# A hybrid transformer block and a PEER block on one core: five weight subtractions moved from VectorE to GpSimd, norms moved later, and fifteen unread float32 products added on TensorE

## The reference, cut to what matters

```python
def reference(x, ...):
    x = first_block(x, ...)
    return second_block(x, ...)

# first_block: rmsnorm, u @ w_in; a gated delta rule with 4 heads in chunks
#   (a triangular solve in each) beside causal attention with 8 heads and a
#   forget gate; @ w_out; a swiglu with d_ff 2816; a last rmsnorm
# second_block:
h = modulate(rmsnorm_2(x, norm1_g), shift1, scale1)
proj = h @ w_in                       # q, k, v, and three inputs of a short convolution
attn = sliding_window_attention(rope(norm(q)), rope(norm(k)), v, sinks)
conv = cb * short_conv(cc * cu, conv_w)
x = x + gate1 * (concat(rmsnorm_2(attn), rmsnorm_2(conv)) @ w_out)
h2 = modulate(rmsnorm_2(x, norm2_g), shift2, scale2)
x = x + gate2 * peer(h2, ...)         # 8 heads, each picks 16 of 16384 experts per token
```

## Time and profile before

| | |
|---|---|
| median of 3 runs | 2389.42 us (2389.01 to 2391.6) |
| profiled execution | 2392.0 us, of which the span from first to last instruction is 2390.2 us |
| busy: PE, DVE, ACT, POOL | 2342.3, 1482.9, 909.6, 1100.0 us |

### The profile page before, as it was taken

One profiled execution on the slowest core, in us unless ns is written; L12 is line 12 of the kernel. 1 busy time (PEld: TensorE's weight loads), 2 busy tenths in 40 slices (PEclk: granted clock), 3 DMA queues, 4 the chain that ended last, 5 costly groups with the idle time before them and its releaser, 6 DMA issues.

```text
span 2390.2 us, 33961 instructions
## 1 busy us (share of the span) xinstructions
PE 2342.3 (98%) x11547; PEld 1490.9 (62%) x11547; DVE 1482.9 (62%) x2863; ACT 909.6 (38%) x1430; POOL 1100.0 (46%) x752
## 2 busy tenths in 40 slices
PE   8999899999999998998999999999999999999999
PEld 6888567668888876645864444444444566666665
DVE  4512367356968557645889885222222499899898
ACT  3222134232232352324345555454545433333332
POOL 0001121010000030002888888888888588886566
PEclk9999899999999999999999999999999999999999
DMA  7240454165656312212446666666667899999997
GB/s 210 71 73 1 155 199 144 70 189 167 210 160 194 88 53 71 71 37 87 89 98 147 157 147 157 146 157 146 157 146 157 276 409 363 373 369 379 369 360 285
DMA packets 437893, 426.51 MB, mean 178 GB/s; under 512 B 105000, under 2 KB 360104, under 8 KB 437680
## 3 DMA queue, kind: packets, MB, share of 16 engines
q1 hardware_dynamic: 353648, 332.85, 43.6%
q0 software_dynamic: 84160, 92.58, 15.5%
HBM read 364.28 MB, written 61.05 MB: 178 GB/s over the span
## 4 chain that ended last, share of the span: by engine, by line
PE 51%; POOL 26%; issue 5%; DVE 4%; ACT 1%; DMA 1%; SPq 0%; DVEq 0%; POOLq 0%; ACTq 0%
POOL dense_gates L868 26%; PE psum L1594 7%; PE psum L1596 7%; PE psum L1595 7%; PE psum L1288 5%; PE psum L1289 5%; PE psum L1290 5%; PE psum L1331 2%; PE psum L1051 1%; PE psum L1175 1%; PE psum L1277 1%; PE psum L1071 1%; PE psum L1131 1%; PE psum L1144 1%; PE psum L1344 1%
## 5 line engine op out<-in xcount | busy, mean ns | idle before, releaser
L868 POOL DMA_INDIRECT dense_gates<-arena x384 | 613.7, 1598 | 122.3 <-issue 116.7
L1571 PE MATMUL psum<-arena 128*128 128x512 bf16 x1024 | 389.8, 381 | 0.0
L1573 PE MATMUL psum<-arena 128*128 128x512 bf16 x1024 | 387.6, 379 | 0.0
L1572 PE MATMUL psum<-arena 128*128 128x512 bf16 x1024 | 387.0, 378 | 0.0
L2722 DVE TENSOR_TENSOR arena<-arena,psum 128x1024 bf16<-128x1024 f32 x124 | 151.5, 1222 | 335.5 <-ACT psum L2003 335.0
L1594 PE MATMUL psum<-arena,low 128*128 128x384 bf16 x1024 | 334.4, 327 | 0.9 <-DVE arena L2756 0.9
L1596 PE MATMUL psum<-arena,low 128*128 128x384 bf16 x1024 | 334.4, 327 | 0.0
L1595 PE MATMUL psum<-arena,low 128*128 128x384 bf16 x1024 | 334.4, 327 | 0.0
L2019 ACT ACTIVATE low<-low 128x1024 bf16<-128x1024 f32 x128 | 135.3, 1057 | 296.4 <-PE psum L1596 281.6
L888 POOL DMA_INDIRECT arena<-in_v,arena x128 | 182.8, 1428 | 75.9 <-DVE arena L2773 43.8
L896 POOL DMA_INDIRECT arena<-gelu_spill,arena x128 | 189.4, 1480 | 59.0 <-issue 36.6
(11 more groups left out here) (409 smaller groups left out, 4104.9 us busy)
## 6 DMA issues: line engine op xcount, KB each, us to landing
arena<-in_uT SPq DMA_DIRECT2D x128, 512.0 KB
low<-in_v SPq DMA_DIRECT2D x128, 512.0 KB, 5.5
gelu_spill<-cst SPq DMA_DIRECT2D x128, 256.0 KB, 3.2
dense_gates<-cst SPq DMA_DIRECT2D x16, 1536.0 KB, 10.3
arena<-in_ada_w POOLq DMA_DIRECT2D x12, 2048.0 KB, 9.0
arena<-gelu_spill SPq DMA_DIRECT2D x128, 192.0 KB, 5.8
arena<-dense_gates SPq DMA_DIRECT2D x128, 192.0 KB, 6.9
low<-in_w_in SPq DMA_DIRECT2D x20, 1024.0 KB, 7.3
```

The costliest lines, as they stand in the source:

```text
L868: pool.indirect_dma_start(gate_cells, bass.IndirectOffsetOnAxis(ap=cell_of[:, n:n + 1], axis=0), gate_of[:, n:n + 1], None, compute_op=ALU ...
L1571: mm(psum[:, bank, :], hi[:, c, :], h2hi[:, c, :], start=c == 0, stop=False)
L1572: mm(psum[:, bank, :], hi[:, c, :], h2lo[:, c, :], start=False, stop=False)
L1573: last = mm(psum[:, bank, :], lo[:, c, :], h2hi[:, c, :], start=False, stop=c == DC - 1)
```

## The change

Two things are changed.

First, `second_low(n)` for n = 0 to 4 goes from DVE to POOL: two ahead of POOL's operand lows and three behind them. PE waits for these on the semaphore g_rhs instead of x_nrm, whose count for n from 5 on is smaller by 5. On DVE the reciprocal of the last norm goes into step 1 of the window loop, and the eight `last_norm` calls go, two by two, into steps 2 to 5, each behind the step's last softmax instruction and ahead of its `second_low` calls.

Second, `keep_busy(bank, count, src)` issues `count` float32 products of 128x128 by 512 columns on constants (or on a tile of zeros at the first place) into a bank that is free there. Nobody reads them. There are six places: 3 behind the first `mean_square`; 1 ahead of item 4 and 2 ahead of item 5; 3 ahead of `first_pair`; 2 ahead of `half_mix`; 4 ahead of the PEER queries.

```diff
-            return S[name], {"x_exp": STEPS, "x_nrm": STEPS, "l2_sq": 2 * GH, ...
+            return S[name], {"x_exp": STEPS, "x_nrm": STEPS - 5, "g_rhs": 3 * NT, "l2_sq": 2 * GH, ...
...
@@ gpsimd
+            def second_low(n):
+                pool.wait_ge(*second_part("x_exp", n + 1))
+                pool.tensor_tensor(second_cols(n, slot_halves), second_cols(n, slot), s_high[n % 4], ALU.subtract
+                                  ).then_inc(S["g_rhs"], 1)
+            for n in range(2):
+                second_low(n)
             for c in range(LOWS_POOL):
                 pool.wait_ge(*second_part("l2_sq", c + 1))
                 pool.tensor_tensor(s_operand_low[c], u2[:, c, :], s_operand_high[c], ALU.subtract).then_inc(S["g_nm"], 1)
+            for n in range(2, 5):
+                second_low(n)
...
@@ tensor
+            def keep_busy(bank, count, src=cst[:, 0:SEC]):
+                for _ in range(count):
+                    mm(psum[:, bank, :], src[:, 0:P], src, start=True, stop=True)
...
             mean_square(0, HALF, [psum[:, 6, 0:HALF], psum[:, 7, 0:HALF]])
+            keep_busy(4, 3, gates[:, 0:SEC])
...
                 if what == "level" and a < len(ITEMS):
+                    if a in (4, 5):
+                        keep_busy(7, a - 3)
                     merge_p(a)
...
             mean_last(0, sq1, "sq1_ready", 0)
+            keep_busy(7, 3)
...
-                pe.wait_ge(*second_part("x_nrm", n + 1))
+                pe.wait_ge(*second_part("x_nrm" if n >= 5 else "g_rhs", n + 1))
...
             pe.wait_ge(*fill_done(F_OUT2))
+            keep_busy(2, 2)
...
             mean_last(3, u2)
+            keep_busy(7, 4)
...
@@ vector
             modulated(0, col_n1, DC)
-            for n in range(2):
-                second_low(n)
...
-            dve.wait_ge(S["std_ready"], 5)
-            settle(dve.reciprocal(r2[:, 1, :], r2[:, 1, :]))
...
-                if j < 4:
-                    last_norm(2 * j)
-                    last_norm(2 * j + 1)
-                if j == 0:
-                    second_low(2)
-            second_low(3)
-            second_low(4)
             rotate(4)
             second_low(5)
...
+                if s == 1:
+                    dve.wait_ge(S["std_ready"], 5)
+                    settle(dve.reciprocal(r2[:, 1, :], r2[:, 1, :]))
+                elif 2 <= s <= 5:
+                    last_norm(2 * s - 4)
+                    last_norm(2 * s - 3)
```

More of the change, by code:

```diff
@@ L451, in second_part @@
         def second_part(name, n):
-            return S[name], {"x_exp": STEPS, "x_nrm": STEPS, "l2_sq": 2 * GH, "l2_done": 2 * GH, "g_nm": len(ITEMS)}[name] + n
+            return S[name], {"x_exp": STEPS, "x_nrm": STEPS - 5, "g_rhs": 3 * NT, "l2_sq": 2 * GH, "l2_done": 2 * GH, "g_nm": len(ITEMS)}[name] + n
         def second_done(n):
```

## The result

The changed kernel took 2372.97 us (median of 4 runs, 2370.54 to 2374.15) against 2389.22 us for the kernel before (4 runs): ratio 0.9926, 95% interval 0.9911 to 0.9942. A second measurement gave 2372.72 us, ratio 0.9932 (0.9917 to 0.9948), where the kernel before took 2388.13. So it is faster, by 15 to 16 us. The profiled execution took 2370.54 us, 21.5 us less than the profiled one of before (2392.0). Why one pair of profiles says 21.5 and the medians say 16.3 is the main question of what follows.

The account below looks back on a forecast made before the run. PE bounds the kernel through a few waits and the clock falls around them (57 us at the lower clock). Terms sum to -23.6 us: 2392.0 profiled gives 2368.4, less 2.6 for the median 2365.8 us; range 2361 to 2380.

Parts of the forecast that it names:

- From profile to median: Last step of the sum: the median of plain runs lies 2.6 us below the profiled execution, so 2368.4 becomes 2365.8.
- Inversion, -12.9: Attention steps around items 4 and 5: with gaps filled the clock no longer falls, saving 12.9 us.
- rival 1: Clock falls in the inversion all the same, behind the unfilled 2.7 us gap; time 2378.7 us; chance 0.15.
- Start, -0.3: Kernel start: filler keeps the clock up, but weights still loading decide; gain 0.3 us, bounds -1.8 and 0.
- Relief, -9.6 (5.7, 1.9, 0.8, 1.2): Second block: wait before product 3 (5.7), its clock fall (1.9), second (0.8) and first (1.2) waits at L1361 shrink.
- the term of -1.2: First wait at L1361, 2.3 us: middle taken between full gain and none if POOL's lows 0 and 1 stop DVE.
- Rival 2: The next wait takes up the relief; only some 3 of 9.6 us come; 2372.4 us; chance 0.13.
- Window loop, 0: Second block's window loop: added reciprocal and norms stand behind the instruction PE waits for; cost 0.
- L1480, -1.8: Half mixes' gap: filling it saves half of 3.6 us at the lower clock, 1.8 us.
- L1506, 0: PEER queries and behind: PE's gain is waited away, since POOL's indirect-write queue does not move with PE's clock; 0.
- The last phase, +1.0: L1594: a gap of some 3 us may let the clock fall; priced +1.0 us, between 0 and 1.9.
- the prediction's own signs: Right: full clock 260 to 440, no L1344 wait above 1 us, last phase 24 us earlier; wrong: stretched u2, POOL waits.

Follow-up runs that it names:

- the fillers alone: Kernel before with unread products added only ahead of items 4 and 5 of the inversion (1 and 2): 2384.15 us, ratio 0.9973.
- the kernel with two lows back: Changed kernel with low parts 0 and 1 of the second block back on VectorE, 2 to 4 staying on POOL: 2369.73 us, ratio 0.9920.
- the norms alone: Changed kernel with all five low parts back on VectorE; reciprocal and norms stay in the window loop, all fillers stay: 2375.16 us, ratio 0.9941.
- The third profile of before: Kernel before, unchanged, run a third time for one more profile: 2385.9 us at clock 0.993.
- the five low parts alone: Changed kernel with reciprocal and eight norms back in the query and key rounds; low parts stay on POOL, fillers stay: 2381.20 us, ratio 0.9965.
- the kernel with the relief only: Changed kernel without any unread products; only low parts, reciprocal and norms moved: 2378.93 us, ratio 0.9954.

## Why the prediction was right, and what it missed

Predicted 2365.8 us, range 2361 to 2380; measured 2373.0. The direction and range hold, and the forecast gains 7 us too much. Against the profiled execution the sum was nearly right: 2368.4 forecast, 2370.5 measured. That it comes within 2.1 us is partly luck: to the first attention scores and through the inversion 2.5 us less were gained than forecast, in the relief 1.4 and in the window loop 0.9 less, ahead of the first write 0.7 more and behind it 2.0 more.

- **From profile to median.** This is the largest miss, 5.0 of the 7.2 us. The prediction took 2.6 us off, as if the changed kernel's median lay under its profile as the old one's did. The profile of before (2392.0) had the longest stretch at half clock of the three, the very thing that the change removes; the changed kernel's profile was the fastest of its four. How long that stretch is in the typical execution is not on record. The medians say what its cure is worth: 6.5 us alone, and all fillers on top of the relief bring 6.0 (2378.93 to 2372.97). A gain that removes a varying loss must be sized on the typical execution.
- **Inversion, -12.9.** Measured -11.1 in the ten steps of the pair and -0.9 in item 5's first products just ahead of them, and 1.7 lost again at 265 behind the gap without a filler, which rival 1 had named; but there the clock was back before 270.6, where a score product takes 1.12 us as before, so rival 1's price was wrong. At the median the fillers alone brought 6.5.
- **Start, -0.3.** About -0.4: the merge at 256.59 before stands at 256.18 after, though the clock is 1.00 from 20 to 40. Right, and leaving it out costs nothing that could be measured.
- **Relief, -9.6 (5.7, 1.9, 0.8, 1.2).** Measured -8.2. The 5.7 us wait and its fall went. The collision was as feared: both low parts stopped u2 (6.70 against 3.26 us), the first turn waits 1.8 of its 2.3 us, and 1.1 us of idle PE is new in the first products, so the term of -1.2 measured +0.6. By the exclusion rule of the Trainium skill (SBUF - State Buffer, "Who interferes with whom") the term was 0 instead of -1.2; the trace and the kernel with two lows back agree with it. Rival 2, that the next wait eats most of it, did not come.
- **How the relief is split.** The prediction gave the low parts 7.6 of the 9.6 us, as if by themselves. Alone they bring nothing (66.6 against 65.3), while the norms alone, priced at the other 2.0, bring 4.3.
- **Window loop, 0.** It is 109.1 against 108.2, and 108.2 to 108.3 in every profile with the norms outside the loop. The reciprocal and norms there cost PE 0.9 us, not 0. Its waits for the convolution's DVE instruction (L2532, L2516 before) are 1.1 us instead of 0.4.
- **L1480, -1.8, and L1506, 0.** "To first write" gained 2.5 in the pair: PE reached the last sum of the norm before PEER (L1262, L1280 after) 56.7 us after its first half mix before and 55.0 after (1.7), so 0.8 came behind it. In the profile of before POOL's first low part for PEER's operand (L861) waits for PE's query products (L1506), so PE's clock moves that queue a little, which the prediction denied. The third profile of before takes 93.3.
- **The last phase, +1.0.** PE waits 1.9 there as foreseen, with no fall in the changed kernel's profile; in that pair "end" gained 1.7. It is 520.3 to 523.8 across the profiles, so this says nothing of the change.

The pair sums to +0.3 - 11.1 + 0.1 - 8.2 + 0.9 - 2.5 + 0.7 - 1.7 = -21.5 us.

Of the prediction's own signs, three came: no wait above 1 us at L1363 (the longest is 0.7), a mean clock near 0.997 (0.999), and a first indirect write that moves with PE (1139.0 to 1118.5). Three did not: the clock is 0.91 in 260 to 280, the last phase starts 21.5 us earlier and not 24, and PE waits 1.9 us there and not 2 to 4. One sign of being wrong came as well, u2 instructions of up to 2.22 us with PE waiting inside L1389 (L1370 before). The product that the prediction calls L1360 stands at L1363.

## What to carry to other kernels

Before pricing a loss of the clock, take two or three profiles of the same kernel: where the loss varies, one profile sizes one execution. Fill the gap behind which the clock stays down long (here one of 2.3 us, with two products); fillers at five other places (start, item 2, item 4, first product, queries) brought nothing that could be measured, and the one ahead of the half mixes was not tried alone. Of work moved off a busy engine, measure each piece alone and look for the next wait on the same engine: here the five low parts alone gave nothing, the norms alone 4.3 us of the relief stretch, both 8.2, and both but two lows 10.6. Start nothing on POOL beside DVE instructions that PE waits for.

## What the runs showed of the hardware

- A gap of the same 2.72 us ahead of the same products let the clock fall in eight of the thirteen profiles that leave it open (5.21 to 5.81 us for the sixteen records) and not in the other five (3.73). A single profile cannot say that a gap is harmless.
- Where a gap was filled, no profile has a fall behind it; where it was open, many have. Start: 5 of 6 open, 0 of 8 filled. Item 5: 4 of 4, 0 of 10. First product of the second block: 4 of 6, 0 of 8. Half mixes: 2 of 5, 0 of 9. Queries: 6 of 6, 0 of 8. What a fall costs is another matter: the relief stretch is 57.2 us in the kernel with the relief only, with the clock at 0.91 in 860 to 880 behind the first product's gap, and 57.2 in the changed kernel, with 1.00 there.
- In two profiles the clock fell at 340 to 360 (0.83) where PE was 19.7 and 19.8 of 20 us busy. What starts a fall there stays open; no experiment was aimed at it.
- Between POOL and DVE the hold-up goes beyond u2: one DVE instruction of a rotation that takes 0.68 us took 2.17 beside POOL's fifth low part, in the changed kernel and with two lows back alike, without PE waiting for it.
